# High and low parts of X and Y at another place in SBUF, 1728 bytes further on

## The reference

```
h = x
h = h + hybrid_mixer(rmsnorm(h))            # SSD scan and stick-breaking attention
h = h + memory_cross_attention(rmsnorm(h), mem)
h = h + square(relu(rmsnorm(h) @ w_ff1)) @ w_ff2          # 4096 hidden features
x = rmsnorm(h)
x = x + conformer_conv(rmsnorm(x))
x = x + conv_ffn(rmsnorm(x))                # 2816 hidden features
x = x + nsa_attention(rmsnorm(x))
x = x + conv_ffn(rmsnorm(x))
```

## Time and profile before

| | us |
|---|---|
| median of 3 runs | 1074.56 (1074.09 to 1076.3) |
| the profiled execution, its own time | 1075.33 |
| its span, first to last instruction | 1073.3 |
| TensorE busy with matmuls in the span | 1038.2 (97%), 8495 matmuls |
| VectorE, ScalarE, GpSimd busy | 753.0, 525.8, 145.1 |
| mean granted TensorE clock | 0.990 of full speed |

### The profile page before, as it was taken

The page is one execution under the profiler, slowest core; times in us unless marked ns, Lnnn a source line. Parts: engine busy times, 40 slices in busy tenths (PEclk is TensorE's granted clock), DMA queues, the critical chain, the costliest instruction groups (busy, mean ns, idle before and its releaser), DMA issues. The chain is left out here.

```text
span 1073.3 us, 22384 instructions
## 1 busy us (share of the span) xinstructions
PE 1038.2 (97%) x8495; PEld 984.0 (92%) x8495; DVE 753.0 (70%) x1209; ACT 525.8 (49%) x900; POOL 145.1 (14%) x194
## 2 busy tenths in 40 slices
PE   9999889799999999998999999999998999999998
PEld 8999669699999998877999999999986699999998
DVE  5866758665666556884877777778867677767775
ACT  6443646554444446225644444465746555444442
POOL 0070010011222110002000000040114600010000
PEclk9999989999999999999999999999999999999999
DMA  9563216256555664650555555556730045555561
GB/s 347 159 188 97 81 38 197 79 162 192 193 184 180 191 193 122 201 162 23 178 196 193 179 193 195 178 153 166 250 118 21 1 129 186 196 188 183 178 196 58
DMA packets 51042, 169.72 MB, mean 158 GB/s; under 512 B 5664, under 2 KB 10784, under 8 KB 50848
## 3 DMA queue, kind: packets, MB, share of 16 engines
q1 hardware_dynamic: 45216, 163.22, 47.4%
q10 hardware_dynamic: 5760, 5.57, 2.0%
HBM read 162.15 MB, written 1.05 MB: 152 GB/s over the span
## 5 line engine op out<-in xcount | busy, mean ns | idle before, releaser
L1534 DVE TENSOR_TENSOR WL<-WR,WH 128x1024 fp32r<-128x1024 f32 x302 | 372.6, 1251 | 146.8 <-ACT WH L1270 143.6
L854 PE MATMUL acc<-XH,WH 128*128 128x256 f32 x1392 | 401.4, 288 | 3.3 <-DVE XP L1551 1.7
L856 PE MATMUL acc<-XH,WL 128*128 128x256 f32 x1392 | 393.4, 283 | 0.0
L855 PE MATMUL acc<-XL,WH 128*128 128x256 f32 x1392 | 393.0, 282 | 0.0
L1270 ACT ACTIVATE WH<-WR 128x1024 fp32r<-128x1024 f32 x302 | 312.3, 1050 | 114.4 <-PE acc L856 80.8
L854 PEld LDWEIGHTS acc<-XH,WH 128*128 128x128 f32 x1392 | 266.0, 191 | 7.1 <-DVE WL L1534 3.9
L855 PEld LDWEIGHTS acc<-XL,WH 128*128 128x128 f32 x1392 | 266.1, 191 | 0.8
L856 PEld LDWEIGHTS acc<-XH,WL 128*128 128x128 f32 x1392 | 266.1, 191 | 0.0
L854 PE MATMUL big<-UH,WH 128*128 128x256 f32 x608 | 168.7, 277 | 0.3 <-POOL UL L2043 0.3
L855 PE MATMUL big<-UL,WH 128*128 128x256 f32 x608 | 168.3, 277 | 0.0
L856 PE MATMUL big<-UH,WL 128*128 128x256 f32 x608 | 168.0, 276 | 0.0
(11 more groups left out here) (286 smaller groups left out, 1234.0 us busy)
## 6 DMA issues: line engine op xcount, KB each, us to landing
WR<-weights SPq DMA_DIRECT2D x302, 512.0 KB, 3.6
STK<-UP ACTq DMA_DIRECT2D x32, 138.0 KB, 3.6
X<-x_t SPq DMA_DIRECT2D x4, 256.0 KB, 5.9
MEM<-mem_t SPq DMA_DIRECT2D x1, 1024.0 KB, 9.6
result_t<-X SPq DMA_DIRECT2D x4, 256.0 KB, 2.2
CON<-constants SPq DMA_DIRECT2D x1, 880.0 KB, 12.4
CBUF<-KCV ACTq DMA_DIRECT2D x4, 128.0 KB, 5.4
CBUF<-KCV ACTq DMA_DIRECT2D x4, 127.5 KB, 6.4
```

Source lines behind the costliest of these rows:

```text
L854: pe.matmul(out, wh, hi, start=start, stop=False, skip_group_check=True)
L855: pe.matmul(out, wh, lo, start=False, stop=False, skip_group_check=True)
L856: return pe.matmul(out, wl, hi, start=False, stop=stop, skip_group_check=True)
L1534: dve.tensor_tensor(WL[:, cs % SPL], WR[:, cs % RAW], WH[:, cs % SPL].bitcast(F32), ALU.subtract).then_inc(w_low, 1)
```

## The change

A tensor of 432 float32 (1728 bytes) that nothing uses is placed ahead of XH, and one of 80 (320 bytes) behind YL. XH, XL, YH and YL, and with them the views ZH and ZL, move up by 1728 bytes; all that comes after them moves by 2048 bytes. No instruction is added, removed or moved.

```diff
         SQ = sb("SQ", [P, KD, T])
+
+        sb("shift", [P, 432])
         XH, XL = sb("XH", [P, KD, T], F32R), sb("XL", [P, KD, T], F32R)
         YH, YL = sb("YH", [P, KD, T], F32R), sb("YL", [P, KD, T], F32R)
+        sb("shift_back", [P, 80])
         WR = sb("WR", [P, RAW, CH])
```

## The result

The changed kernel takes **1066.39 us** (median of 4 runs, 1061.16 to 1067.29) against 1075.43 for the kernel before beside it: a ratio of **0.9901** with a 95% interval of 0.988 to 0.9922. It is faster by 1.0%, where 2.9% was forecast; the forecast of 1043.6 us with its range up to 1061 is missed. Run again, in six more executions, the ratio was 0.9898 (0.9863 to 0.9933).

The account below looks back on a forecast made before the run. TensorE's matmul start-to-start distance was taken as the bound. Gains 9.8 + 16.6 + 5.1 + 1.5 less 1.9 gave 31.1 us, so 1043.6 us against the median of 1074.56; 8-in-10 range 1039 to 1061.

Parts of the forecast that it names:

- What bounds the kernel: Whole kernel: TensorE, busy 97% of the span, holds back the weight stream; the distance between matmul starts counts.
- The cause of 113.3 against 120.0: U's matmuls against X's: the moving operand's place modulo 2048 sets the rate, 113.3 or 120.0 ns each.
- the rows of `out_half`: Trace rows: 12 matmuls at 120.0 ns despite fewer slice changes and more bank changes, taken to leave place as cause.
- The 109 ns: Estimate for any 256-column matmul from the skill page's 2.5 ns above the columns; the rows had 113.3 and 120.0.
- Moving X: X's 174 chunks at U's rate, 2.72 us each: 9.8 us from tiles after a `wide`, 16.6 us from the others.
- a cost that would go, 1.5 us: U behind X: each `wide` starts with three matmuls at the slower rate; removing this gains 76 x 0.02 us.
- the 19.3 us for the feed-forward parts: Share of the 31 us gain expected in the three feed-forward parts, which hold 120 of X's 174 tiles.
- Moving Y and the X of the mixers: Mixers: Y's 32 chunks gain 0.16 us each, 5.1 us; with X's tiles there, the rest beyond 19.3 of 31 us.
- The loaded operand, the other engines, the weight stream: `token_part` and `compress` loads taken as 0 (-1.6 to +1.6 us); other engines' accesses hidden, cost nothing; no weight DMA late.
- Half of it: Rival, chance 0.10: X and Y meet in another phase, near 116.7 ns per matmul; about 1060 us.
- No effect: Rival, chance 0.10: `acc` banks or one slice serving 24 matmuls set the rate, not place; time stays 1074.6 us.
- slower: Rival, chance 0.06: the new place is worse for each `tile`, 126.7 ns per matmul, 33 us more, 1107 us.

## Why the prediction was wrong, point by point

**What bounds the kernel** was right: TensorE's distance from start to start. Wherever it fell, the time followed, by up to 24 us, with no new wait behind it.

**The cause of 113.3 against 120.0** was half right. The place of the moving operand matters, as the rows of `out_half` had left it; its distance from the weights is what acts. The Trainium skill ("TensorE: Matmul & The Clock Gate", Step-by-step: what each phase is for) says that TensorE reads the streaming and the loaded operand through two independent ports, so that the next load takes no read bandwidth from the running matmul; in these runs the distance between the two is worth up to 6.7 ns in 120. The 109 ns that the prediction worked out is by that page's figure for a matmul by itself; for pairs of load and matmul the same section (Back-to-back issue gap) lets both set the distance, so the gap from 109 to 113.3 says nothing against it.

**Moving X, the step that failed:** "If they run as U does, a chunk takes 24 x 113.3 = 2.72 us." U's 113.3 was not a property of its place. It was the quick one of two states there, and U was in it because every `wide` came out of a chunk at 120.0. The change took away that neighbour: U fell back to 117.7 together with X. The row was in view: the first three matmuls of each `wide` were at 120, and only then came 113.3. I read this as a cost that would go, 1.5 us; it was the run-in that made the quick state. Measured in place of the 19.3 us for the feed-forward parts: a loss of 2.1. That the neighbour did it is shown by U at 0, which gave X its 113.3, and by the 12 matmuls at distance 0, which gave it to X and U. It isn't the only way in: behind some waits and breaks the quick state came without it.

**Moving Y and the X of the mixers:** 11.8 us of the sum were theirs; 10.2 and 6.1 were measured in two profiles that differ in their clock. The 10.2 come close only by luck, since some 5 of them are the clock. There the state is chosen anew at every break and comes out at either rate: Y of the last attention at 113.3, other tiles at 117.7.

**The loaded operand, the other engines, the weight stream** were rightly left at about nothing: no wait of theirs grew to note.

**The rivals.** "Half of it" had the 117.7 right to a nanosecond and X in it, with 1060 us at a chance of 0.10; what it lacked is U's loss. "No effect" and "slower" fall. No case had the moved part harm one that wasn't touched. The direction, faster, was right.

## What to carry to other kernels

When two rates of one instruction stand side by side, read how each begins before giving it to a place or a shape: a rate that sets in only some matmuls behind another kind is a state, and changing its neighbour can take it away. A layout is then judged by whole loops, not by one operand, and a few matmuls of run-in, or a layout with every streaming operand 192 bytes from the weights modulo 256, can be worth 2%. Where times scatter after a change of layout only, read the profile for such states before timing more.

## What the runs showed of the hardware that was not expected

- fp32r matmuls of 256 columns with a 128-column load each had distances from 113.3 to 120.0 ns at 2.4 GHz, by the distance of the two operands modulo 256 bytes: 120.0 at 0, 113.3 or 117.7 at 192 and at 64. At the clock of 1.2 GHz the one stretch read, at a distance of 0, has no such loss: 213.3 ns.
- At one distance (192 modulo 256) two states exist. Each was kept over more than 1500 matmuls, a whole feed-forward part in which no matmul came late. Behind one plain float32 matmul the quick state was lost in all three parts of one run. Behind starts that came 0.16 to 0.73 us apart, with no plain matmul, the other state came at several places; behind others, such as 0.16 us at 693.03 in the run with 12 extra matmuls, the state stayed.
- Six to twelve matmuls at a distance of 0 led to the quick state in every part of the profiles taken (three parts in each). Three led to it in none of three, nor did twelve at the same distance as the tile behind them.
